# Two-block transformer kernel: gate strips and convolution taps moved from the projection stage into the sparse attention

## What is computed

```
h = rms_norm(x);  proj = h @ w_in                    # 1024 -> 4504 columns
q, k/v (three kinds), gates, z_nsa, u_lru, z_lru, glu_a, glu_b, z_conv = split(proj)
y_nsa  = sparse attention with three branches (compressed, selected, window), gated
y_lru  = linear recurrence over tokens of u_lru (conv of 4 taps, two gates, scan)
u      = glu_a * sigmoid(glu_b);  u = causal depthwise conv of 31 taps
y_conv = silu(layer_norm(u)) @ w_pw2
x = x + concat(y_nsa*silu(z_nsa), y_lru*silu(z_lru), y_conv*silu(z_conv)) @ w_out
```

## Time and profile before

| | us |
|---|---|
| median of 3 runs (lowest, highest) | 2529.61 (2525.16, 2539.0) |
| the profiled execution | 2528.15 |
| its span on the core | 2526.4 |
| PE busy | 2309.7 (91%) |
| DVE busy | 1371.4 (54%) |
| ACT busy | 1103.2 (44%) |
| POOL busy | 864.3 (34%) |

### The profile page before, as it was taken

One profiled execution on the slowest core, in us unless ns is written; L12 is line 12 of the kernel. 1 busy time (PEld: TensorE's weight loads), 2 busy tenths in 40 slices (PEclk: granted clock), 3 DMA queues, 4 the chain that ended last, 5 costly groups with the idle time before them and its releaser, 6 DMA issues.

```text
span 2526.4 us, 33893 instructions
## 1 busy us (share of the span) xinstructions
PE 2309.7 (91%) x12078; PEld 1840.7 (73%) x12078; DVE 1371.4 (54%) x3026; ACT 1103.2 (44%) x2322; POOL 864.3 (34%) x664
## 2 busy tenths in 40 slices
PE   7899889999988898888989999999977998999998
PEld 6677666777766687666877888877755787788886
DVE  6988774388778626856553212235566565320222
ACT  5432465354137643736454323333444645332332
POOL 5433203454221152022324545542200232554553
PEclk9999879999988799889999999999978999999998
DMA  4224002332410031111313333333101131333332
GB/s 157 75 77 131 18 1 63 86 94 71 129 43 6 19 115 43 35 42 47 112 51 88 97 105 99 93 85 98 62 11 41 57 109 51 92 93 101 98 93 71
DMA packets 105414, 187.03 MB, mean 74 GB/s; under 512 B 11424, under 2 KB 22688, under 8 KB 104992
## 3 DMA queue, kind: packets, MB, share of 16 engines
q1 hardware_dynamic: 99504, 175.91, 23.9%
q10 hardware_dynamic: 5744, 8.95, 1.1%
HBM read 182.71 MB, written 2.10 MB: 73 GB/s over the span
## 4 chain that ended last, share of the span: by engine, by line
PE 72%; DVE 18%; issue 4%; ACT 4%; DMA 0%; SPq 0%; POOL 0%; DVEq 0%; ACTq 0%
PE bank L727 18%; PE bank L728 18%; PE bank L729 18%; PE bank L893 5%; PE bank L914 4%; PE bank L905 4%; DVE bank L1734 3%; DVE temp L1636 2%; ACT op_hi L1019 1%; DVE conv_area L1340 1%; PE bank L786 1%; DVE temp L1386 1%; DVE temp L1591 1%; DVE temp L1405 1%; DVE temp L1620 1%
## 5 line engine op out<-in xcount | busy, mean ns | idle before, releaser
L1879 POOL TENSOR_TENSOR w_lo<-w_raw,w_hi 128x512 fp32r<-128x512 f32 (+2 forms) x620 | 834.7, 1352 | 1567.0 <-ACT w_hi L1015 1566.6
L727 PE MATMUL bank<-op_hi,w_hi 128*128 128x512 f32 x1840 | 742.3, 403 | 30.9 <-DVE op_lo L1331 24.3
L728 PE MATMUL bank<-op_lo,w_hi 128*128 128x512 f32 x1840 | 722.5, 393 | 0.0
L729 PE MATMUL bank<-op_hi,w_lo 128*128 128x512 f32 x1840 | 722.5, 393 | 0.0
L1015 ACT ACTIVATE w_hi<-w_raw 128x512 fp32r<-128x512 f32 (+2 forms) x636 | 383.5, 614 | 712.7 <-PE bank L729 710.2
L727 PEld LDWEIGHTS bank<-op_hi,w_hi 128*128 128x128 f32 x1840 | 349.5, 190 | 121.8 <-issue 17.6
L728 PEld LDWEIGHTS bank<-op_lo,w_hi 128*128 128x128 f32 x1840 | 349.5, 190 | 78.0 <-issue 7.8
L729 PEld LDWEIGHTS bank<-op_hi,w_lo 128*128 128x128 f32 x1840 | 348.7, 189 | 74.6
L1386 DVE TENSOR_TENSOR temp<-bank,rstd 128x512 f32<-128x512 f32 (+1 forms) x159 | 109.9, 691 | 388.5 <-PE bank L729 373.1
L1453 DVE TENSOR_TENSOR x_t<-bank,x_t 128x512 f32<-128x512 f32 x80 | 55.3, 691 | 376.5 <-PE bank L729 376.5
L727 PE MATMUL bank<-side_hi,w_hi 128*128 128x512 f32 (+2 forms) x632 | 240.5, 380 | 3.3 <-DVE side_lo L1331 2.9
(11 more groups left out here) (221 smaller groups left out, 2583.2 us busy)
## 6 DMA issues: line engine op xcount, KB each, us to landing
w_raw<-in_weights SPq DMA_DIRECT2D x618, 256.0 KB, 2.7
w_raw<-in_weights SPq DMA_DIRECT2D x34, 192.0 KB, 2.3
conv_area<-in_bias ACTq DMA_DIRECT2D x2, 1920.0 KB, 8.5
x_t<-in_x SPq DMA_DIRECT2D x8, 256.0 KB, 5.6
conv_area<-in_mem ACTq DMA_DIRECT2D x2, 1024.0 KB, 5.4
out_y<-ybuf SPq DMA_DIRECT2D x8, 256.0 KB, 2.1
temp<-in_lru_w ACTq DMA_DIRECT2D x2, 512.0 KB, 8.1
cos_t<-in_extra ACTq DMA_DIRECT2D x3, 256.0 KB, 3.2
```

The costliest lines, as they stand in the source:

```text
L727: pe.matmul(dst, w[0], m[0], start=start, stop=False)
L728: pe.matmul(dst, w[0], m[1], start=False, stop=False)
L729: return pe.matmul(dst, w[1], m[0], start=False, stop=stop)
L1879: pool.tensor_tensor(w_lo[:, j, 0:n], w_raw[:, p % RAW_RING, 0:n], w_hi[:, j, 0:n].bitcast(F32), ALU.subtract).then_inc(*mark("weights_spl ...
```

## The change

- The eight strips z_lru and z_conv of a layer leave part A. They form a part Z, whose 16 pieces run inside PE's attention list at the steps of `FILL_STEPS` (two of three steps, 3 to 26 of 48), each after the values of its step. DVE takes each strip out two items after its last piece. z_lru goes to two new buffers `zl`; the recurrence writes `ybuf` directly, and silu and product follow in two batches (`z_silu`, items 31 and 56). ACT splits these pieces inside the attention.
- `TAPS`: 19 taps in part A, 69 in part B, 36 in the attention (items 3 to 50, three of four items). The taps of the attention, and the last of part B, keep their running sum in `acc` in SBUF.
- Layer norm moves from items 8 to 47 to items 55 to 85 (its silu and split stay).
- Score banks: in the sparse attention 2, 3, 7, and 1 too from tile 60 on; in all others 1, 2, 3, 0. The sparse attention has one output bank, 6, so that the first values of a group wait for the output of the group before.
- In all attentions `normed` lags two items behind `maxed` instead of one, and DVE's part of `split`, `ln_split` and `z_silu` comes two items after ACT's.

```diff
-TAPS = {"A": [0, 0, 0, 0, 3] + 3 * [6, 1, 6, 1, 3],
-        "B": [5, 0, 5, 1, 5, 1, 1, 0, 4, 1, 5, 1, 5, 1, 5, 2, 5, 5, 6, 6, 6]}
+TAPS = {"A": [0, 0, 1] + 3 * [0, 5, 1],
+        "B": [5, 0, 5, 1, 5, 1, 1, 0, 4, 1, 5, 1, 5, 1, 5, 2, 5, 5, 6, 6, 5],
+        "NSA": [0, 0, 0] + 12 * [1, 1, 1, 0]}
+FILL_STEPS = [3, 5, 6, 8, 9, 11, 12, 14, 15, 17, 18, 20, 21, 23, 24, 26]
...
-            for kind in ("z_lru", "u_lru", "glu_b", "glu_a", "z_conv"):
+            for kind in ("u_lru", "glu_b", "glu_a"):
...
+        for kind, c in [(k, c) for half in (0, 2) for k in ("z_lru", "z_conv") for c in (half, half + 1)]:
+            add(("Z", l), kind, c, "w_in", l, COLS[kind] + P * c, DC, ("h1", l))
...
+                    banks = (1, 2, 3, 0) if not nsa else (2, 3, 7) if at_tile - ts[0]["a"] < LN_TILES else (2, 3, 7, 1)
+                    t["out"] = 6 if nsa or at_group % 2 == 0 else 7
...
-                at(8, "ln_sum", l)
-                at(10, "ln_mean", l)
-                at(12, "ln_spread", l)
+                at(31, "z_silu", l, 0)
+                at(56, "z_silu", l, 1)
+                at(55, "ln_sum", l)
+                at(57, "ln_mean", l)
+                at(59, "ln_spread", l)
+                at(75, "ln_var", l)
+                at(77, "ln_factor", l)
+                at(80, "ln_spread_factor", l)
...
-                        if t["first"] and t["g"] >= 2:
-                            pe.wait_ge(*after("outputs_taken", t["g"] - 2))
+                        if t["first"] and t["emptied"] is not None:
+                            pe.wait_ge(*after("outputs_taken", t["emptied"]))
...
+                    if i in FILL_AT.get(part, ()):
+                        p = FILL_AT[part][i]
+                        strip(PIECES[p].strip.n, False, {}, p)
...
-                    settle(dve.tensor_tensor_scan(xc, la, lr, 0.0, ALU.mult, ALU.add))
-                    dve.wait_ge(*after("z_silu", n - 1))
-                    settle(dve.tensor_tensor(ybuf[:, 4 + c, :], xc, ybuf[:, 4 + c, :], ALU.mult))
+                    settle(dve.tensor_tensor_scan(ybuf[:, 4 + c, :], la, lr, 0.0, ALU.mult, ALU.add))
...
-                    if 1 <= i < len(ts) + 1:
-                        normed(ts[i - 1])
+                    if NORM_LAG <= i < len(ts) + NORM_LAG:
+                        normed(ts[i - NORM_LAG])
...
+                    for stage in between.get(i - LOW_LAG, ()):
+                        if stage[0] in ("split", "ln_split", "z_silu"):
+                            extra_stage(*stage)
...
+                    taps(part, i)
```

More of the change, by code:

```diff
@@ L525, in build @@
                     t["first"], t["last"] = t["pos"] == 0, t["pos"] == t["size"] - 1
+                    nsa = step[1][0] == "NSA"
+                    banks = (1, 2, 3, 0) if not nsa else (2, 3, 7) if at_tile - ts[0]["a"] < LN_TILES else (2, 3, 7, 1)
+                    t["out"] = 6 if nsa or at_group % 2 == 0 else 7
+                    t["emptied"] = emptied.get(t["out"])
+                    if t["last"]:
+                        emptied[t["out"]] = at_group
+                    t["bank"] = banks[(at_tile - ts[0]["a"]) % len(banks)]
+                    t["held"] = held.get(t["bank"])
+                    held[t["bank"]] = at_tile
                     at_tile += 1
@@ L530, in build @@
                 ATT[step[1]] = ts
+        FILL, FILL_AT = {}, {}
+        for l in range(LAYERS):
+            FILL["NSA", l] = part_range(STRIPS, ("Z", l))
+            ps = [p for n in FILL["NSA", l] for p in STRIPS[n].pieces]
+            FILL_AT["NSA", l] = {2 * s: p for s, p in zip(FILL_STEPS, ps)}
         ENDS = 0
@@ L546, in build, with fill_done @@
                 used[SLOT_OF[p]] = p
+        def fill_done(part, i):
+            p = FILL_AT.get(part, {}).get(i - 2)
+            return None if p is None or PIECES[p].strip.pieces[-1] != p else PIECES[p].strip.n
         def last_of(n):
@@ L757, in factor_spread, with strip @@
                     ins.then_inc(*mark("first_spread", 0))
-            def strip(n, fresh, between):
+            def strip(n, fresh, between, only=None):
                 s = STRIPS[n]
-                if n >= 2:
+                if n >= 2 and only in (None, s.pieces[0]):
                     pe.wait_ge(*after("strip_taken", n - 2))
                 dst = bank[n % 2][0:s.out, 0:s.cols]
-                for p in s.pieces:
+                for p in s.pieces if only is None else (only,):
                     k0, m, w = PIECES[p].k, PIECES[p].m, PIECES[p].w
@@ L885, in scores @@
                     for t in pair:
-                        a = t["a"]
-                        if a >= SCORE_BANKS:
-                            pe.wait_ge(*after("maxed", a - SCORE_BANKS))
+                        if t["held"] is not None:
+                            pe.wait_ge(*after("maxed", t["held"]))
+                        if part[0] == "NSA" and t["a"] == ts[LN_TILES]["a"]:
+                            pe.wait_ge(*after("strip_taken", FILL[part][-1]))
                     for x, y in ((0, 0), (0, 1), (1, 0)):
@@ L953, in extra_stage @@
                 if kind in ("ln_sum", "ln_var"):
+                    if kind == "ln_sum":
+                        pe.wait_ge(*after("strip_taken", FILL["NSA", l][-1]))
                     pe.wait_ge(*after("ln_added" if kind == "ln_sum" else "ln_squares", l))
@@ L1194, in attend @@
                 for i in range(len(ts) + OUT_LAG + 1):
-                    if i == OUT_LAG + 3:
+                    if i == (max(FILL_AT[part]) + 4 if part in FILL_AT else OUT_LAG + 3):
                         split_to(last_of(FOLLOWS[part]))
+                    if part in FILL_AT and i == 0:
+                        split_to(STRIPS[FILL[part][0]].pieces[-1])
                     if 2 * TURN_LAG <= i < len(ts) + 2 * TURN_LAG:
@@ L1200, in attend @@
                         exps(ts[i])
+                    if i in FILL_AT.get(part, ()):
+                        split_to(min(FILL_AT[part][i] + 2, last_of(FILL[part][-1])))
                     for stage in between.get(i, ()):
@@ L1206, in extra_stage @@
                 if kind == "split":
+                    if l[0] == "mix" and c == 0:
+                        act.wait_ge(*after("weights_used", last_of(FILL["NSA", l[1]][-1])))
+                    if l[0] == "mix" and c < 4:
+                        act.wait_ge(*after("z_mixed", (l[1], c)))
                     split(l, c)
+                elif kind == "z_silu":
+                    for n in FILL["NSA", l][4 * c:4 * c + 4]:
+                        evac(n)
                 elif kind == "ln_factor":
@@ L1664, in output @@
                     dve.wait_ge(*after("values", t["a"]))
-                    o = bank[6 + g % 2][:, 0:P if w == HD else 2 * P]
+                    o = bank[t["out"]][:, 0:P if w == HD else 2 * P]
                     if t["gate"] is not None:
@@ L1687, in extra_stage @@
                     low(l, c, mixed(l, c))
+                elif kind == "z_silu":
+                    for n in FILL["NSA", l][4 * c:4 * c + 2]:
+                        y = ybuf[:, 4 + STRIPS[n].idx, :]
+                        dve.wait_ge(*after("z_silu", n))
+                        dve.tensor_tensor(y, y, zl[STRIPS[n].idx % 2], ALU.mult).then_inc(*mark("z_mixed", (l, STRIPS[n].idx)))
+                        dve.wait_ge(*after("z_mixed", (l, STRIPS[n].idx)))
                 elif kind == "ln_mean":
@@ L1871, in layer_norm @@
                     ins.then_inc(*(mark("ln_pool") if a + b != 2 else mark("ln_squares", l)))
-            ends = {part_range(STRIPS, ("B", l))[-1]: l for l in range(LAYERS)}
+            ends = {part_range(STRIPS, ("Z", l))[-1]: l for l in range(LAYERS)}
             for p, q in enumerate(PIECES):
```

68 lines of the change are left out of this document (40 added, 28 removed).

## The result

The changed kernel takes 2541.11 us (median, 2537.5 to 2543.64), the kernel before, run beside it on the same chip, 2531.4. The ratio is 1.0033, interval [1.0024, 1.0042]. So it is 0.33% slower, clear of noise but under the bound of 0.5% that I had set for a difference; the forecast of 2510 and "faster" was wrong, while the range held the time. The medians are 9.7 us apart.

A forecast was written before the change was run, and what follows sets the result against it. PE was taken to bound the kernel, busy 2309.7 of 2526.4 us, with DVE work mattering where it releases PE. Per layer -42 - 0.8 + 36.5 = -6.3; twice that and -6 is -18.6, giving 2510 us, range 2478 to 2548.

The forecast's parts named there:

- Part A: Stage ahead of the sparse attention, taken as DVE-bound: saves 42 us a layer, bounds 38 and 46; chunks of 20.3 us.
- First half of the attention: Sparse attention up to group 8's output: grows by 32 us a layer, bounds 26 and 45, at 12.1 us a group.
- The work terms: Work per group in the sparse attention's first half: PE 10.8 us at full clock, DVE 10.6 with POOL's contention.
- friction: Time PE and DVE lose by meshing badly in the sparse attention's first half: 1.4 us a group above their work.
- The output bank: Single bank in the sparse attention, PE's values waiting for DVE's output: 0.4 us a group while DVE is on time.
- Second half: Sparse attention after group 8's output: grows by 4.5 us a layer, including 6 for layer norm.
- the credits: Savings expected in the sparse attention's second half: -4 for the split stall, -4 for fourth score bank and lag.
- The split stall: Sparse attention's second half: DVE's 7.9 us wait for ACT largely goes with the lag of two, -4 us.
- Other attentions: All attentions but the sparse ones: fourth score bank and lag save 6 us in all, bounds -14 and +4.
- rival C: Rival, 17%: sparse attention's single output bank locks PE and DVE together, pieces and taps add; growth 55 a layer, 2550 us.
- A: Rival, 25%: the sparse attention takes most of the fill in its idle time; growth 24 us a layer, 2482 us.
- B: Rival, 18%: the sparse attention gives back just what part A saves, by contention and late DVE; growth 42, 2524 us.

## Why the prediction was wrong

**Part A: right.** -42.8 a layer with the tap of B, measured -38.5, near the lower bound; chunks of 19.9 and 21.8 for 20.3, DVE busy for 60.1 of the 65 us from 541 to 606. PE is busy for 60.5 of them, so both engines now fill the stage. The stage fell short where PE came late (9.06 us at the start). 9 us of the miss.

**First half of the attention: right in kind, short in size.** +37.2 for +32, 12.76 us a group for 12.1. The work terms held: by the busy shares of the first window PE works 11.6 us a group at a clock of 0.93, which is 10.7 at full clock where 10.8 was forecast, and DVE 10.2 where 10.6 was, POOL's hits included. The port did as the rule said (the Trainium skill, "SBUF — State Buffer", Who interferes with whom: a DVE instruction with two SBUF inputs contends with GpSimd reading SBUF): 1.80 against 0.74 us on a hit. But taking the subtractions away gave 3 to 5 us a layer where I had counted 7, half a hit for each of the 16; one hit for each, the pessimistic reading, is further off. What was too small is the friction, 1.4 a group forecast and 2.1 measured (12.76 - 10.7). Its parts by the runs: output behind the maximum and piece ahead of the scores, 11 us over the half. The output bank was priced at 0.4 a group; PE stands 0.57 to 0.78 for it. I had reasoned that the pieces cover friction as independent work. They did not, because PE is in order: a piece ahead of the scores is a 2.7 us delay to DVE's next maximum. 10 us of the miss.

**Second half: the step that failed.** +4.5 forecast, +18.0 measured, 27 us over both layers and the largest miss. "Layer norm now lies here ... 0.8 x 7 = 6 for it" was a difference between the halves' intervals in the kernel before; but the other half carries the splits, so it priced layer norm minus splits. With layer norm left out, it measures 12.7 here and 14 in its old place (there the groups come 6.4 us apart without it, not 8.3). That is half of this miss.

The other half is in the credits: without layer norm this half still takes 66.5 us where it took 60.5 in the old kernel without it (65.5 and 61.6 in layer 1), and by the forecast's other terms it should have been 1.5 shorter. The split stall of 7.9 us was read as lying at items 66 to 69. Only 2.6 us of it did, and they are gone. The rest is a wait at the last splits, behind the layer norm's silus, and it stays; before and after:

```profile
401.75 1.29 DVE L1329 TENSOR_TENSOR op_lo<-conv_area,op_hi 128x512 fp32r<-128x512 f32 x2 [5.26 <-ACT op_hi L1019]
```

```profile
420.93 1.29 DVE L1383 TENSOR_TENSOR op_lo<-conv_area,op_hi 128x512 fp32r<-128x512 f32 x2 [4.92 <-ACT op_hi L1056]
```

The lag of two gave next to nothing (a lag of one leaves the time as it was); the fourth score bank of this half had no run of its own. The second silu batch cost 3.8 / 2.2 us rather than 2. And the mean clock, 0.86 in my rows, is 0.69: 435 matmuls are busy for 64.0 us, 0.147 each, where 401 took 47.7, 0.119 each. Without layer norm it is 0.79. That the low clock follows from PE's waits for ACT and DVE is my reading; no run holds the clock and changes the waits.

**Other attentions: twice to three times too small.** -6 forecast, -18 in the traces and -21 as a run by itself, past the bound of -14. I allowed 28 us of idle time in 291 and took a fifth. Cut exactly, it was 31.6 in 289.4, a small error. The larger one: PE's busy time fell too, from 257.8 to 246.3, which I had taken as fixed. 12 us the other way.

9 + 10 + 27 - 12 = 34, the distance from -18.6 to +15.2 of the profiled executions; between the medians it is 28. That the time lies inside the range is luck: 2541 was to come by rival C alone, and it is the gain in the other attentions, three times the forecast, that keeps it under 2548.

**The rivals.** C had the number, a growth of 55, and its mechanism is there but too small to carry it: PE does wait for an output in nearly every group, yet below the 1 us that I had named as a sign of being wrong, the first half came to 12.76 us a group and not 14, and taking the output first is worth 7 a layer. C put 9 us into the second half, which grew by 18. The longest waits of the kernel after in the first half, then the second:

```profile
ACT temp L1233 <- PE bank L937: 35.4, 17, 4.7
ACT temp L1222 <- DVE small L1690: 17.5, 21, 2.3
DVE temp L1690 <- issue: 13.4, 7, 4.3
```

```profile
DVE temp L1690 <- PE bank L925: 15.4, 12, 4.5
PEld bank L937 <- issue: 9.6, 12, 3.6
```

They are the circle of scores, maximum, exponential and transposes, each late for the next. Leaving layer norm out takes 12.7 us of that away in the second half, and right orders take 11 away in the first. A fails by the same figures; that B's growth of 42 is what the kernel with both orders has is a coincidence, since B put it down to contention.

**What stays open.** The 19 us a layer that by the estimate come with the strips whatever their length, in the first half. In the kernel with strips only, both orders take 7 of them away (105.3 to 98.3). POOL's port took 3 in this half of the changed kernel (110.3 to 107.4), with the taps in; the silus took nothing there. Some 9 to 12 stay unexplained, and no run has all of these together. Open too: the 4 to 6 us by which the second half without layer norm is longer than in the old kernel.

## What to carry to other kernels

Before filling an engine's slack, see what it is made of. In the first half of the old attention PE was busy for 64 of 73 us at a mean clock of 0.76, so the room was mostly a low clock and not idle time. Filler put there cost most of its own length (0.63 us per us of matmul, and by estimate 19 us a layer beside), while the place it left gave 38.5 us only because DVE's taps left with it; with the taps kept there it gave 21 to 25. And filler goes behind the instruction that the next engine waits for, never ahead of it. Price a step that is moved by leaving it out at both ends, not by comparing stretches that carry different things: 13 us of layer norm a layer looked like 6. When a change has several edits, time the smallest by itself: the bank and the lag alone gave 21 us, which the rest ate. And where an instruction starts right behind another that it depends on, at every place alike, believe the times over the name that the list of waits gives: PE's wait for the output bank stood there as a wait for ACT's copy.

## What was unexpected of the hardware

The granted clock of PE is far from full in stretches where PE shows 80% busy: its mean is 0.69 in the second half after (busy 64 of 79 us), 0.79 with layer norm gone (52 of 65), 0.93 in the first half where pieces fill it (100 of 111). Two thirds of the pieces' matmuls taken away cost clock, from 0.93 to 0.79, and gave back only 18.4 us of 29. A tap of 0.74 us takes up to 1.80 beside a subtraction of POOL, and a division of 0.55 up to 1.65, yet 16 subtractions cost no more than 3 to 5 us of a layer. And 36 taps, 28 us of DVE work a layer, cost 1 to 2 us beside the strips in both orders but 16 to 21 without strips: here, work on the second engine was nearly free once the first one was the slower.
